# A hybrid decoder step: the FFN as one long up projection by seven block products for eight, activations through DRAM, and then a down projection in four blocks

## The chip, the cores and the metric

One Trainium2 chip, one core. The metric is the device time of one execution in microseconds. The kernel before takes 1333.52 us (median of 3 runs, 1333.43 to 1334.73).

## The reference, cut to what matters

One decoder layer over 16 meta tokens, 1024 prompt tokens and 8 x 4 sample tokens. The change is in its last two lines, the feed-forward network (FFN):

```python
D_MODEL = 1024; FFN_HIDDEN = 4 * D_MODEL          # all arrays float32
h = h + jnp.concatenate([y_a, y_b], axis=-1) @ w_out
u = jax.nn.relu(rmsnorm(h, norm_ffn) @ w_up)      # (tokens, 1024) @ (1024, 4096)
h = h + (u * u) @ w_down                          # (tokens, 4096) @ (4096, 1024)
y = rmsnorm(h, norm_final)                        # meta tokens dropped
```

Everything ahead of it (convolutions, gated delta rule, the product with `w_out`) is not touched, but for how the `w_out` stage hands `h` on.

## The kernel before, in words

Features lie on the 128 partitions, tokens along the free dimension: 1056 kept token columns (`KEPT`), or two halves of 528 (`HALF`), each of two parts of 264 (`PART`). A float32 product is made of three matmuls: every operand is split into a high part rounded to `float32r` (ScalarE, a copy) and a low part, the rest (a subtraction on VectorE or GpSimd), and TensorE adds high x high, high x low and low x high in PSUM. Each matmul has its own 128x128 weight load.

- `out_rows` (VectorE, L2611 on) adds the `w_out` product to `h` (`hT`), squares it into `h_squares`, and makes the low part `hg_low` of h times the norm's gain; `out_high` (ScalarE, L1297) makes `hg_high`.
- `sum_h` (TensorE, L1911), after the first unit of the FFN, adds the squares over the partitions into two banks for three column groups, so that its third group waits for VectorE's first `rstd_mid` (L2644). Then follow a square root (ScalarE L1309) and a reciprocal (VectorE L2647).
- Up projection (`up`, L1927 to L1929): 32 tiles of 128 hidden features, each over three column groups (288, 384, 384), 8 k-tiles x 3 matmuls in each. `up_rows` (VectorE, L2655, L2657) reads the bank, scales it by `h_squares`, and makes relu squared into `u_row`. 
- Down projection (`product`, L1945 to L1947): for 7 of 8 blocks of 4 hidden tiles it is done by Strassen-Winograd products: seven products instead of eight for each pair of output tiles (`PRODUCTS`; operands S of the weights, T of the activations). GpSimd makes the S sums (`pair_low`, L973 to L980) and the T sums (`make_t`, L954 to L960), ScalarE the high parts (L1325, L1334), VectorE the T low parts (L2661), GpSimd the weights' (L947, L966). `product_rows` (VectorE, L2676) adds each product to `hT`, 10 reads for 7 products. The last block goes without block products (`last_down`, L1963 to L1965), interleaved with transposes for the output.
- Order: each engine runs one list written out by hand. TensorE: up of blocks 0 and 1, then by turns the down products of block b and the up tiles of block b + 2 (`for b in range(NB - 1)`). Nothing of `u` leaves the chip's SBUF. SyncE's queue loads the weights, 512 KB each, through a ring; w_high and w_low hold eight sets of down weights.
- Counts in `acc_done`, `acc_read_dve`, `w_high`, `w_low` say when a unit's matmuls are done, a bank is read, and a weight set is ready; a queue waits in its order, and what stands behind a waiting instruction waits too.

Of the kernel before, what the change touches and what calls it, by code (L numbers as in the profile page):

```python
# [7 lines left out]
ALU = mybir.AluOpType  # L8
ACT = mybir.ActivationFunctionType
AX = mybir.AxisListType  # L10
F32 = mybir.dt.float32
# [34 lines left out]
FB = 4  # L46
NB = FFN // (FB * P)
HALF, PART = KEPT // 2, KEPT // 4
PAIRS = D // (2 * P)
PRODUCTS = [("A11", "B11", ((0, 0, 1), (1, 1, 1))), ("A12", "B21", ((0, 0, 1),)), ("S1", "T1", ((1, 0, -1), (1, 1, 1))),  # L50
            ("S2", "T2", ((1, 1, 1),)), ("S3", "T3", ((0, 1, -1), (1, 1, 1))), ("S4", "B22", ((0, 1, 1),)),
            ("A22", "T4", ((1, 0, 1),))]
READS = [len(x[2]) for x in PRODUCTS]
NP = len(PRODUCTS)
OPS = ("B11", "T1", "B21", "B22", "T2", "T3", "T4")
# [45 lines left out]
def build(nc, x_prompt, x_sample, state_conv_a, state_conv_qkv, state_ssm, meta_tokens, norm_mix, w_in,  # L101
# [4 lines left out]
    with ctx:  # L106
# [42 lines left out]
        hg_h = place("hg_high", [P, KT, TOK], F32R, R1)  # L149
        hg_l = place("hg_low", [P, KT, TOK], F32R, R1 + KT * SLOT)  # L150
        OPB = 2 * (FB // 2) * HALF * 4
        op_h = {x: place(f"op_high_{x}", [P, FB // 2, HALF], F32R, RK + OPB * i) for i, x in enumerate(OPS)}
        op_l = {x: place(f"op_low_{x}", [P, FB // 2, HALF], F32R, RK + OPB * i + OPB // 2) for i, x in enumerate(OPS)}
# [3 lines left out]
        w_pair = [place(f"w_pair{i}", [P, FB, 2 * P], F32, RING + 4096 * i) for i in range(2)]  # L157
# [103 lines left out]
        def scratch(name, shape):  # L261
# [8 lines left out]
        gate_d = scratch("gate_kept_rows", [NH, P, TOK])  # L270

# [3 lines left out]
        hsq = place("h_squares", [P, TOK], F32, RZ + NT * P * 4)  # L275
        ROW = KEPT * 4
        u_row = [place(f"u_row{i}", [P, KEPT], F32, a) for i, a in enumerate(
            [RK + NP * OPB, RK + NP * OPB + ROW, FREE, FREE + ROW, FREE + 2 * ROW, RZ])]
        assert NP * OPB + 2 * ROW <= 16 * SLOT and ROW <= NT * P * 4
        s_tmp = [place(f"w_sum{i}", [P, FB // 2, P], F32, FREE + 3 * ROW + 1024 * i) for i in range(2)]  # L280
        assert FREE + 3 * ROW + 2048 <= R1

        u_h = place("u_last_high", [P, FB, KEPT], F32R, R1)
        u_l = place("u_last_low", [P, FB, KEPT], F32R, R1 + FB * ROW)
# [98 lines left out]
        def has_last(n):  # L383
            return IN_TILES[n][0] in ("k", "q", "v", "H")

        N_LAST = sum(has_last(n) for n in range(N_IN))
        PER_UP, PER_DOWN = 3 * FB, NP * PAIRS
        DONE0, READ0 = 3 * N_MIX, dve_reads_to(N_MIX)

        def up_unit(b, i, m):  # L390
# [2393 lines left out]
```

## Time and profile before

| | us |
|---|---|
| median of 3 runs (lowest, highest) | 1333.52 (1333.43, 1334.73) |
| profiled execution: span, first to last instruction | 1329.9 |
| median less that span | 3.6 |
| FFN up to the first `last_down` matmul | 606.75 to 1267.62 |
| PE busy / DVE / POOL / ACT in the span | 1313.7 / 839.3 / 524.3 / 412.2 |

No time of its own is recorded for the profiled execution beyond its span; the runs are 3.6 us longer. Start times of rows are microseconds from the first instruction. A matmul's duration in a row is longer than its step to the next one, since matmuls overlap; the step between starts is what counts. A row's idle time is what its engine waited ahead of it. A row of windows reads: stretch, its length, busy time and instruction count of PE, PEld, DVE, ACT and POOL, granted clock, DMA share, GB/s. A row of groups reads: line, engine, operation, tiles, shape, count, busy us, mean ns, idle us ahead and what ended it. A row of a timeline reads: start, duration, engine, line, operation, tiles, shape, count.

### The profile page before, as it was taken

How to read it: one execution, taken by the hardware profiler on the slowest of the kernel's cores; microseconds unless marked ns; L12 is line 12 of the kernel's file. 1: busy time of each engine (PE TensorE's matmuls, PEld its weight loads, DVE VectorE, ACT ScalarE, POOL GpSimd, SP SyncE). 2: the span in 40 equal slices, each digit the busy share in tenths (PEclk: the TensorE clock that was granted, in tenths of full speed). 3: DMA queues.
4: the chain of work that ended last, by engine and by line, in shares of the span. 5: the costliest groups of instructions: out<-in, count | busy, mean ns of one | idle time of the engine just before them, and what ended most of it. 6: DMA issues, size and time to landing. Idle time of an engine off the chain costs nothing.

```text
span 1329.9 us, 22476 instructions
## 1 busy us (share of the span) xinstructions
PE 1313.7 (99%) x8984; PEld 1282.4 (96%) x8984; DVE 839.3 (63%) x1415; ACT 412.2 (31%) x806; POOL 524.3 (39%) x544
## 2 busy tenths in 40 slices
PE   7999999999999999999999999999999999999997
PEld 6899999899999999999999999999999999999997
DVE  6567898336453665556666756756667567566866
ACT  7566642112222213232122222322222223222313
POOL 1322112111111211221367466574574755746811
PEclk9999999999999999999999999999999999999999
DMA  6223554533323323221111212112121121111213
GB/s 193 71 66 90 163 179 77 185 115 88 88 64 85 99 57 90 81 65 48 48 33 48 64 33 63 34 48 64 33 59 54 34 63 48 49 49 32 81 39 124
DMA packets 161946, 99.88 MB, mean 75 GB/s; under 512 B 19735, under 2 KB 156467, under 8 KB 161842
## 3 DMA queue, kind: packets, MB, share of 16 engines
q1 hardware_dynamic: 138866, 85.56, 22.0%
q10 hardware_dynamic: 22976, 12.88, 3.6%
q8 instruction: 72, 1.18, 0.4%
q14 instruction: 32, 0.26, 0.1%
HBM read 77.62 MB, written 20.80 MB: 74 GB/s over the span
## 4 chain that ended last, share of the span: by engine, by line
PE 94%; DVE 3%; ACT 1%; issue 1%; DMA 1%; SPq 0%; POOLq 0%; POOL 0%; DVEq 0%; ACTq 0%
PE banks L1401 10%; PE banks L1403 9%; PE banks L1402 9%; PE banks L1927 9%; PE banks L1929 9%; PE banks L1928 9%; PE banks L1946 7%; PE banks L1947 7%; PE banks L1945 7%; PE banks L1963 1%; PE banks L1964 1%; PE banks L1965 1%; PE banks L1621 1%; PE banks L1635 1%; PE banks L1857 1%
## 5 line engine op out<-in xcount | busy, mean ns | idle before, releaser
L1927 PE MATMUL banks<-hg_high,w_high 128*128 128x384 f32 (+1 forms) x768 | 249.5, 325 | 0.0
L1929 PE MATMUL banks<-hg_high,w_low 128*128 128x384 f32 (+1 forms) x768 | 247.6, 322 | 0.0
L1928 PE MATMUL banks<-hg_low,w_high 128*128 128x384 f32 (+1 forms) x768 | 247.3, 322 | 0.0
L2676 DVE TENSOR_TENSOR hT<-hT,banks 128x528 f32<-128x528 f32 x280 | 189.4, 701 | 84.0 <-PE banks L1947 76.8
L1401 PE MATMUL banks<-xn_high,w_high 128*128 128x384 f32 (+1 forms) x672 | 227.3, 338 | 1.0 <-DVE xn_low L2059 0.9
L1403 PE MATMUL banks<-xn_high,w_low 128*128 128x384 f32 (+1 forms) x672 | 218.6, 325 | 0.0
L1402 PE MATMUL banks<-xn_low,w_high 128*128 128x384 f32 (+1 forms) x672 | 218.4, 325 | 0.0
L821 POOL TENSOR_TENSOR w_low<-w_raw,w_high 128x1024 fp32r<-128x1024 f32 x31 | 77.0, 2483 | 243.6 <-ACT w_high L1015 243.6
L1927 PEld LDWEIGHTS banks<-hg_high,w_high 128*128 128x128 f32 x768 | 144.2, 188 | 1.9 <-POOL w_low L947 1.7
L1928 PEld LDWEIGHTS banks<-hg_low,w_high 128*128 128x128 f32 x768 | 144.3, 188 | 0.1
L1929 PEld LDWEIGHTS banks<-hg_high,w_low 128*128 128x128 f32 x768 | 144.2, 188 | 0.0
L1401 PEld LDWEIGHTS banks<-xn_high,w_high 128*128 128x128 f32 x672 | 126.9, 189 | 3.6 <-DVE xn_low L2059 1.1
L966 POOL TENSOR_TENSOR w_low<-w_pair,w_high 128x256 fp32r<-128x256 f32 x140 | 104.1, 761 | 66.3 <-ACT w_high L1334 66.3
L2655 DVE TENSOR_TENSOR u_row<-banks,h_squares 128x384 f32<-128x384 f32 (+1 forms) x96 | 50.1, 522 | 126.4 <-PE banks L1929 126.2
L947 POOL TENSOR_TENSOR w_low<-w_raw,w_high 128x1024 fp32r<-128x1024 f32 x31 | 78.3, 2526 | 126.9 <-ACT w_high L1316 126.9
L1947 PE MATMUL banks<-op_high_T,w_low 128*128 128x264 f32 x448 | 127.7, 285 | 0.0
L1946 PE MATMUL banks<-op_low_T,w_high 128*128 128x264 f32 x448 | 127.7, 285 | 0.0
L1402 PEld LDWEIGHTS banks<-xn_low,w_high 128*128 128x128 f32 x672 | 127.2, 189 | 0.0
L1945 PE MATMUL banks<-op_high_T,w_high 128*128 128x264 f32 x448 | 127.1, 284 | 0.0
L1403 PEld LDWEIGHTS banks<-xn_high,w_low 128*128 128x128 f32 x672 | 126.6, 188 | 0.0
L1334 ACT ACTIVATE w_high<-w_pair 128x256 fp32r<-128x256 f32 x140 | 55.5, 415 | 177.5 <-PE banks L1929 84.3
L1947 PE MATMUL banks<-op_high_B,w_low 128*128 128x264 f32 x336 | 95.8, 285 | 0.0
(334 smaller groups left out, 2779.4 us busy)
## 6 DMA issues: line engine op xcount, KB each, us to landing
w_raw<-in_w_up SPq DMA_DIRECT2D x32, 512.0 KB, 4.1
w_pair<-in_w_down SPq DMA_DIRECT2D x32, 512.0 KB, 3.4
w_raw<-in_w_in SPq DMA_DIRECT2D x28, 512.0 KB, 4.0
w_raw<-in_w_out SPq DMA_DIRECT2D x8, 512.0 KB, 4.2
x_slice<-in_x_prompt SPq DMA_DIRECT2D x8, 512.0 KB, 4.3
out<-y_tok SPq DMA_DIRECT2D x8, 512.0 KB, 2.7
v_kept_rows<-v_feat SPq DMA_DIRECT2D x4, 536.0 KB, 2.9
gate_kept_rows<-gate_row SPq DMA_DIRECT2D x4, 536.0 KB, 3.3
```

What stands on the lines that cost most here:

```text
L947: pool.tensor_tensor(w_l[half][:, :, :], w_raw[n % 2][:, :, :], w_h[half][:, :, :].bitcast(F32), ALU.subtract).then_inc(w_low, 1)
L966: pool.tensor_tensor(set_of(w_l, b, s), set_source(n, PRODUCTS[x][0]), set_of(w_h, b, s).bitcast(F32), ALU.subtract).then_inc(w_low, 1)
L1401: pe.matmul(bank[:, 0:w], w_h[n % 2][:, k, :], hi[:, c0:c0 + w], start=(k == first), stop=False)
L1402: pe.matmul(bank[:, 0:w], w_h[n % 2][:, k, :], lo[:, c0:c0 + w], start=False, stop=False)
L1403: ins = pe.matmul(bank[:, 0:w], w_l[n % 2][:, k, :], hi[:, c0:c0 + w], start=False, stop=(k == last))
L1927: pe.matmul(bank[:, 0:w], w_h[half][:, k, :], hg_h[:, k, c0:c0 + w], start=(k == 0), stop=False)
L1928: pe.matmul(bank[:, 0:w], w_h[half][:, k, :], hg_l[:, k, c0:c0 + w], start=False, stop=False)
L1929: ins = pe.matmul(bank[:, 0:w], w_l[half][:, k, :], hg_h[:, k, c0:c0 + w], start=False, stop=(k == KT - 1))
L1945: pe.matmul(bank, high[:, j, :], op_h[name][:, j, cols], start=(j == 0), stop=False)
L1946: pe.matmul(bank, high[:, j, :], op_l[name][:, j, cols], start=False, stop=False)
L1947: ins = pe.matmul(bank, low[:, j, :], op_h[name][:, j, cols], start=False, stop=(j == FB // 2 - 1))
L2676: dve.tensor_tensor(hc, hc, both, ALU.add if sign > 0 else ALU.subtract).then_inc(acc_read_dve, 1)
```

## The change

Two phases. Up: all 16 pairs of hidden tiles by seven block products each (four k-tiles deep, 24 matmuls of 264 columns). Operands of h are made once at the start: `B11`, `B21`, `B22`, `T1` in the `w_out` stage, `T3`, `T2`, `T4` in turn after it, while pairs 0 and 1 run in the interleaved order `U_SEQ`. The results of pairs 0 to 13 are scaled, squared (ScalarE), turned into the seven operands of the down projection (VectorE) and sent to DRAM (SyncE). Down: block 0 of two pairs, blocks 1 to 3 of four, each product reading its operand back; pairs 14 and 15 stay and go to `last_down`. Weight sets: four, of up to four tiles, instead of eight of two.

```diff
+BLOCKS = ((0, 2), (2, 4), (6, 4), (10, 4))
+U_SEQ = ([(0, 0), (0, 1), (1, 0), (1, 1), (0, 4), (1, 4), (0, 6), (1, 6), (0, 2), (1, 2), (0, 3), (1, 3), (0, 5), (1, 5)]
+         + [(c, x) for c in range(2, UP_PAIRS) for x in range(NP)])
+FIRST_BANKS = (0, 1, 2, 3, 0, 2, 0, 2, 0, 2, 0, 2, 1, 3)
+CHAIN_BANK = (0, 1, 2, 3, 0, 1, 2)
+D_SEQ = ([(0, x, pair) for pair in range(PAIRS) for x in range(NP)]
+         + [(b, x, pair) for b in range(1, len(BLOCKS)) for x in range(NP) for pair in range(PAIRS)])
...
+        def set_free(s):
+            return DONE0 + s - 3 if s >= 4 else 3 * (N_MIX - 1 + s // 2)
...
 SyncE
+            for c in range(UP_PAIRS - 2):
+                send_row1(c)
...
+                send_row0(c)
+                send_turned(c)
+                if 2 <= c < UP_PAIRS - 3:
+                    sp.wait_ge(w_low, low_made(U_UNIT[c + 1, 6]))
+                    load_up(c + 3)
+            kept_pairs_sent()
+            load_part(0, 1)
+            sp.wait_ge(w_low, low_made(U_UNIT[UP_PAIRS - 2, 6]))
+            load_half(0)
+            for x in range(6):
+                load_first_op(x)
+            sp.wait_ge(w_low, low_made(U_UNIT[UP_PAIRS - 1, 6]))
+            load_part(0, 0)
+            load_first_op(6)
...
 GpSimd
+            up_low(1, 3)
+            up_low(0, 5)
+            for j in range(4):
+                turned_low(j)
+            up_low(1, 5)
+            for c in range(2, UP_PAIRS):
+                up_sum(c)
+                up_low(c, 0)
+                up_difference(c)
+                up_low(c, 1)
+                up_less_own(c)
+                for x in (2, 3, 4):
+                    up_low(c, x)
+                up_rest(c)
+                up_low(c, 5)
+                up_low(c, 6)
...
 ScalarE
+            last_half_scaled(0)
+            last_half_scaled(1)
+            up_set_high(1, 0)
+            last_half_scaled(2)
+            last_half_scaled(3)
...
+            up_set_high(1, 3)
+            turned_high("T4", 3)
+            up_set_high(0, 5)
+            up_set_high(1, 5)
...
 TensorE
+            def up(c, x):
+                u, name = U_UNIT[c, x], PRODUCTS[x][1]
+                if c == 0:
+                    if name == "T2":
+                        pe.wait_ge(w_low, low_made(T2_LOWS_AT) - 1)
+                    else:
+                        pe.wait_ge(low_s, UP_LOWS[name])
+                product(u, u, set_h[u % 4], set_l[u % 4], up_h[name], up_l[name], x >= 4 and not (c < 2 and x == 6))
...
 VectorE
+            turned_raw("T3", 0)
+            half_low("B22", N_OUT - 1, 1, 16)
+            turned_raw("T3", 1)
+            up_rows(0, 0)
+            for g in range(3):
+                mean_h(g)
+            up_rows(0, 1)
...
+            up_rows(0, 2)
+            turned_raw("T4", 3)
+            turned_low("T4", 0)
+            up_rows(1, 2)
...
+            root_inverse(2)
+            up_rows(1, 5)
+            right_whole(1)
+            root_inverse(3)
+            scale_row1(0)
+            scale_row0(0)
+            turn_u12(0)
+            turn_u34(0)
+            up_rows(2, 0)
```

`turned_raw` and `turned_low` are two-input operations on 528 columns. `up_rows` reads a product's two banks (528 columns) once, for x = 2 of pairs 0 and 1 twice. `scale_row1` and `scale_row0` take relu times `h_squares`, `turn_u12` and `turn_u34` make four operands of 528 columns. `change_basis` moves to pairs 4 to 7. `turned_low(j)` on GpSimd makes the four low parts of T2, `root_inverse(i)` a quarter of the reciprocal. `turned_low`, `up_low` and `down_low` count in one semaphore, `w_low`; `low_made(T2_LOWS_AT) - 1` is reached when sets 0 to 12 and the four T2 parts are made. Set 12 is that of (0, 5). In the down phase VectorE reads 10 times for seven products in blocks 1 to 3 and 7 times in block 0.

## Rows read from the trace of the kernel before

**Rows 1.** The page, sections 1 and 2: engines' busy time; granted clock by slice.
```profile
span 1329.9 us, 22476 instructions
PE 1313.7 (99%) x8984; PEld 1282.4 (96%) x8984; DVE 839.3 (63%) x1415; ACT 412.2 (31%) x806; POOL 524.3 (39%) x544
PEclk9999999999999999999999999999999999999999
```

**Rows 2.** Busy time by engine: FFN before its last block; one up block; one down block.
```profile
606.75:1267.80 661.05, 661.05 (x4665) 658.44 (x4664) 441.23 (x596) 178.52 (x335) 396.88 (x398) 1.00 0.17 50
742.50:788.95 46.45, 46.45 (x290) 46.20 (x289) 28.96 (x37) 12.89 (x21) 25.94 (x19) 1.00 0.14 43
701.43:742.50 41.07, 41.07 (x337) 41.07 (x337) 27.91 (x41) 10.77 (x25) 28.29 (x37) 1.00 0.19 55
```

**Rows 3.** Timeline of TensorE: matmuls of 384 and 264 columns, where an up block ends.
```profile
701.09 0.34 PE L1928 MATMUL banks<-hg_low,w_high 128*128 128x384 f32 x1
701.26 0.34 PE L1929 MATMUL banks<-hg_high,w_low 128*128 128x384 f32 x1
701.43 0.28 PE L1945 MATMUL banks<-op_high_B,w_high 128*128 128x264 f32 x1
701.55 0.28 PE L1946 MATMUL banks<-op_low_B,w_high 128*128 128x264 f32 x1
```

**Rows 4.** Timeline of TensorE at the FFN's start: the sum of squares.
```profile
609.95 2.11 PE L1911 MATMUL banks<-h_squares,one 128*128 128x288 f32 x6
611.60 0.63 PE L1927 MATMUL banks<-hg_high,w_high 128*128 128x384 f32 x1
```

**Rows 5.** Timeline of VectorE at the FFN's start.
```profile
606.95 0.55 DVE L2619 TENSOR_TENSOR hT<-hT,banks 128x384 f32<-128x384 f32 x1 [2.23 <-PE banks L1403]
608.14 0.56 DVE L2628 TENSOR_TENSOR h_squares<-h_squares,banks 128x384 f32<-128x384 f32 x1
610.63 0.46 DVE L2644 TENSOR_SCALAR h_squares<-banks 128x288 f32<-128x288 f32 x1 [1.41 <-PE banks L1911]
613.81 6.75 DVE L2647 RECIPROCAL h_squares<-h_squares 128x1056 f32<-128x1056 f32 x1 [1.16 <-ACT h_squares L1309]
```

**Rows 6.** Groups by line and shape, VectorE and ScalarE: busy us, mean ns | idle before.
```profile
L2676 DVE TENSOR_TENSOR hT<-hT,banks 128x528 f32<-128x528 f32 x280 | 189.4, 701 | 84.0 <-PE banks L1947 76.8
L2661 DVE TENSOR_TENSOR op_low_B<-u_row,op_high_B 128x528 fp32r<-128x528 f32 x42 | 28.2, 699 | 0.0
L2661 DVE TENSOR_TENSOR op_low_T<-u_row,op_high_T 128x528 fp32r<-128x528 f32 x56 | 81.5, 1476 | 2.8 <-ACT op_high_T L1325 2.8
L1325 ACT ACTIVATE op_high_T<-u_row 128x528 fp32r<-128x528 f32 x56 | 36.2, 647 | 143.4 <-POOL u_row L957 66.3 <-POOL u_row L954 51.1 <-POOL u_row L960 14.5
L1297 ACT ACTIVATE hg_high<-hT,tn 128x384 fp32r<-128x384 f32 x16 | 9.9, 618 | 54.2 <-DVE hT L2619 54.2
```

**Rows 7.** Groups by line and shape, GpSimd.
```profile
L966 POOL TENSOR_TENSOR w_low<-w_pair,w_high 128x256 fp32r<-128x256 f32 x140 | 104.1, 761 | 66.3 <-ACT w_high L1334 66.3
L957 POOL TENSOR_TENSOR u_row<-u_row,u_row 128x528 f32<-128x528 f32 x14 | 18.5, 1323 | 71.8 <-DVE op_low_B L2661 71.8
L960 POOL TENSOR_TENSOR u_row<-u_row 128x528 f32<-128x528 f32 x14 | 24.2, 1727 | 0.0
```

**Rows 8.** Timelines of VectorE and GpSimd: two VectorE additions beside one GpSimd subtraction; one alone.
```profile
633.10 3.52 DVE L2681 TENSOR_TENSOR hT<-hT 128x528 f32<-128x528 f32 x2
633.23 2.82 POOL L947 TENSOR_TENSOR w_low<-w_raw,w_high 128x1024 fp32r<-128x1024 f32 x1 [9.19 <-ACT w_high L1316]
743.90 2.39 POOL L947 TENSOR_TENSOR w_low<-w_raw,w_high 128x1024 fp32r<-128x1024 f32 x1 [3.47 <-ACT w_high L1316]
```

**Rows 9.** DMA: the queue's packets and share; issues with KB and us to landing.
```profile
q1 hardware_dynamic: 138866, 85.56, 22.0%
v_kept_rows<-v_feat SPq DMA_DIRECT2D x4, 536.0 KB, 2.9
x_tok<-in_x_prompt SPq DMA_DIRECT2D x1, 1024.0 KB, 8.3
```

More of the change, by code:

```diff
@@ new lines, in build, with parts_to, op_slot @@
+        for pair in range(PAIRS):
+            for i, name in enumerate(("S1", "S3", "S2", "S4")):
+                S_MADE[0, pair, name] = 4 * UP_PAIRS + 4 * pair + i + 1
+        for b in range(1, len(BLOCKS)):
+            for i, name in enumerate(("S1", "S3", "S2", "S4")):
+                for pair in range(PAIRS):
+                    S_MADE[b, pair, name] = 4 * UP_PAIRS + 4 * PAIRS * b + PAIRS * i + pair + 1
+        def parts_to(b):
+            return sum(n for _, n in BLOCKS[:b + 1])
+        def op_slot(o):
+            return 1 + (o - 1) % 4 if o else 0
@@ new lines, in load_part @@
+            def load_part(b, m):
+                k0, n = BLOCKS[b]
+                dst = ((w_down_12, w_down_22) if b else (w_first_12, w_first_22))[m]
+                sp.wait_ge(w_load[1], (A12_LOADED, A22_LOADED)[m][b] - 16 * n)
+                for j in range(n):
+                    sp.dma_start(dst[:, j, :, :], w_down_part_v[m, :, k0 + j, :, :]).then_inc(w_load[1], 16)
+            sp.wait_ge(w_low, N_MIX)
+            load_up(0)
+            load_up(1)
+            sp.wait_ge(w_low, low_made(U_UNIT[0, 5]))
@@ L998, in _ @@
+            for pair in range(PAIRS):
+                pool.wait_ge(w_high, high_made(LAST0 + pair))
+                pool.tensor_tensor(wx_l[pair][:, :, :], wx_raw[pair][:, :, :], wx_h[pair][:, :, :].bitcast(F32),
                                    ALU.subtract).then_inc(w_low, 1)
@@ L1360, in square_half @@
+            act.wait_ge(w_load[0], WX_LOADED)
+            for pair in range(PAIRS):
+                act.activation(wx_h[pair][:, :, :], wx_raw[pair][:, :, :], ACT.Copy).then_inc(w_high, 1)
             def square_half(r, half):
@@ L2690, in _, with down_rows @@
-            for i in range(FB):
-                for m in range(3):
-                    up_rows(0, i, m)
-                change_basis(i, ALU.subtract)
-            for b in range(NB - 1):
-                for c in range(PER_UP):
-                    up_rows(b + 1, c // 3, c % 3)
-                    if c < 2 * len(LOWS_AT):
-                        for name in LOWS_AT[c % 4]:
-                            op_low(b, c // 4, name)
-                for pair in range(PAIRS):
-                    for x in range(NP):
-                        product_rows(b, pair, x)
-                        if b == NB - 2 and pair and x in (0, 2, 4, 6):
-                            last_u_low(*LAST_LOWS[4 * (pair - 1) + x // 2])
+            def down_rows(b, x, pair):
+                u = D_UNIT[b, x, pair]
+                both = unit_pair(u)
+                dve.wait_ge(acc_done, done(u))
+                for mi, half, sign in (SINGLE_READS[x] if b else (CHAIN_READS[x],)):
+                    hc = split(quarter(pair, mi, half))
+                    dve.wait_ge(acc_read_dve, read(u - 1))
+                    dve.tensor_tensor(hc, hc, both, ALU.add if sign > 0 else ALU.subtract).then_inc(acc_read_dve, 1)
```

968 lines of the change are left out of this document (661 added, 307 removed).

## The prediction, made before the changed kernel ran

> **What bounds the kernel now.** I read the page's busy times first, then who waited for whom on TensorE, then the FFN's windows, then the timelines where stages meet. TensorE is busy 1313.7 of 1329.9 us, the next engine 839.3, and the granted clock is full in every slice [rows 1]. In the FFN up to its last block it is busy in 661.05 of 661.05 us [rows 2]: there the time is the number of matmuls times their step. Nothing else is on the path, so only two things count: how many steps the change removes, and which new waits open. The median is 3.6 us above the profiled span (1333.5 against 1329.9); I add the change to the median.
>
> **The up projection, removed and added.** An up block of four tiles takes 46.45 us [rows 2]; eight are 371.6 us (2304 matmuls of 352 columns on average). A down block of 336 matmuls of 264 columns takes 41.07 us [rows 2], a step of 122.2 ns, as neighbouring starts have it (701.43, 701.55 [rows 3]). The new up stage has 16 pairs x 7 products x 24 = 2688 matmuls of this same form: 328.6 us, 2.93 a product, 20.5 a pair. That is 43.0 us less. The down products are 7 x 28 x 12 before and 28 x 6 x (2 + 4 + 4 + 4) after, 2352 both times, at the same step: 0. The last block is the same: 0.
>
> Steps of 384 columns are 0.17 us, of 264 columns 0.12 [rows 3], so the time goes nearly by columns. The Trainium skill (TensorE: Matmul & The Clock Gate, "Back-to-back issue gap") has a rule that speaks against the change: a stream of weight load and matmul runs at about 81 ns at 128 columns and 131 at 512. An estimate on the line through that page's two figures is 110 ns at 352 columns and 99 at 264, and the up stage would grow by 11 us instead of shrinking by 43. The trace disagrees at both widths.
>
> **The start: three new waits.** Count from S, the first up product (606.75 before). Durations: a VectorE operation on 528 columns 0.70 [rows 6]; a high part on ScalarE 0.65, with a gain 0.75 (0.618 at 384 columns [rows 6], scaled up); GpSimd 1.32 at 528 columns, 0.76 at 256 [rows 7], so 1.29 at 512.
>
> (a) sum_h. Before, VectorE takes up the mean (L2644) 0.68 us after the sum began, and the sum costs TensorE 611.60 - 609.95 = 1.65 us [rows 4, 5]. After, VectorE finishes the last squares at S + 1.95 (608.70 [rows 5]), then has T3's first part (ready for it at S + 2.3, after two ScalarE operations with gain), the last low part of B22, T3's second part and up_rows(0, 0) ahead of the mean: four at 0.70 to 0.76, till S + 5.3. The mean takes 0.46; the third sum starts at 5.8 to 6.3, and the next product at about 6.8 instead of 2.93 + 1.65 = 4.6. Cost 2.2; ends 0 and 4 (all four beside GpSimd).
>
> (b) T2's low parts. Product 10, (0, 3), waits for weight set 12 and behind it four GpSimd operations. From the end of product 8: up_rows(0, 2) reads twice (1.4), T4's last raw part (0.7), its high part on ScalarE (0.65), set 12's high part queued behind it (0.65), its low part (1.3), the four T2 parts (5.3): 10.0 us, plus 0.7 to 1.5 for VectorE's T4 low parts in between (next paragraph). Product 9 covers 2.93. Cost 7.1 to 8.6; I take 7.8. Nothing else covers it: products 11 to 13 stand behind 10 in TensorE's list.
>
> (c) VectorE's backlog after it. Behind up_rows(1, 5) come right_whole (0.7), a quarter of the reciprocal (6.75 / 4 = 1.7 [rows 5]), two scalings of 1056 columns (1.4 each), ScalarE's square (1.1), four turns (2.8), and only then up_rows(2, 0), 10 us if undisturbed; the piece ahead, a quarter of the reciprocal before up_rows(1, 5), adds 0.9. Product (2, 4) needs that bank read, 4 x 2.93 = 11.7 us after product (1, 5). With nothing in the way it just fits (0); with GpSimd in the way of seven operations at 0.6 it is 4 late. I take 2.5.
>
> **The port, or what VectorE and GpSimd share.** Two VectorE additions of two SBUF inputs, 0.70 each undisturbed, take 3.52 beside a GpSimd subtraction that takes 2.82 where it takes 2.39 alone [rows 8]; together they last as long as their sum (3.8). VectorE's T low parts, made while GpSimd works, have a mean of 1.476 against 0.699 [rows 6]; operations with one input in PSUM keep 0.701 with GpSimd busy 28 of 41 us [rows 2, 6]. So these two kinds exclude each other, and their times add. An up pair needs 11 GpSimd operations at 1.29 (14.2) and on VectorE four turns and two scalings (six operations, 4.9): 19.1 of 20.5 us, and 20.5 in pairs 4 to 7 with change_basis. TensorE is not held: a set may be late by three products (8.8) less its own 0.65 and 1.29, 6.9 us. Cost 0; the far end is the third rival.
>
> The Trainium skill (SBUF — State Buffer, "Who interferes with whom") says the same more sharply: with two SBUF inputs on VectorE and a GpSimd read the second to issue is blocked for the other's whole instruction. By it GpSimd would be stopped up to 1.4 us by the long scaling and the pair's sum would stay 19.1; by plain sharing of bandwidth it would be less. The rows fit the rule, and by both TensorE isn't held.
>
> VectorE alone in a pair: seven reads (4.9), 4.9, six waits of up to 1.3: at most 17.6 of 20.5. ScalarE: 7 x 0.65 + 2 x 1.1 = 6.8. SyncE: load_up(c + 3) is queued behind the sends of pair c, which end about product (c + 1, 4); 1 MB lands within 8.3 us [rows 9], still some 10 us before GpSimd wants it. DRAM traffic of a pair is 7 x 0.27 + 1.05 = 2.9 MB in 20.5 us, 141 GB/s; a queue's packets move 85.56 MB in 22.0% of the span, 292 GB/s when all engines move [rows 9]. Hidden.
>
> **The turn to the down phase.** From 3 us before the last pair begins to 12 us into it SyncE issues 5.8 MB (weights of block 0, seven operands of 0.54 MB). At 292 GB/s they end at +17 to +20, and the last operand is wanted by ScalarE at +22, the first at +12. Cost 0; at the slowest rate of [rows 9] (1 MB in 8.3 us, 126 GB/s) it would be 46 us, some 20 late. Nearer is the 536 KB in 2.9 us (189 GB/s): 31 us, hence 5 late. I take 1. Block 1 crowds the port: GpSimd has 8 operations in four products for x = 0, 1, 2, 4 (10.3), VectorE a low part of 2 x 1.4, and in block 1 two scalings (x = 0) and last_u_low (x = 4, 5) besides, so x = 0 needs 15.9 of 11.7 us, x = 1 and 2 13.1 each. The lag grows to 7.0 against the 6.9 allowed. I take 1; ends 0 and 5. Block 0 has GpSimd at 44 x 0.77 = 34 of 41 us as now, with half as many sets ahead (4.4 us less 1.2): 0.
>
> **Sum.** -43.0 + 2.2 + 7.8 + 2.5 + 1 + 1 = -28.5. Time 1305.0.
>
> **Rivals.**
> 1. The waits at the start overlap with what they delay (VectorE catches up during (b), and the backlog (c) and sum_h go away): only (b), 7.1, remains: 1333.5 - 43.0 + 7.1 = 1297.6; with nothing at all 1290.5. For it: VectorE idles for 8 us in (b). Against: (c) comes after, and depends on (b)'s products, not on work that could be done in (b).
> 2. The turn or block 1 costs much more: 5 and 5 instead of 2, up to 20: 1313 to 1323. For it: SyncE's list waits in order; the trace never shows 5.8 MB at once. Against: 292 GB/s in the packets.
> 3. Slower: the port binds the whole up stage. If GpSimd's 11 operations last 1.67 (1.727 at 528 columns [rows 7]) and VectorE's 4.9 still come on top, a pair takes 23.3 us, 2.8 over TensorE, in 14 pairs 39 us: 1305.0 + 39 = 1344. It decides from 2.0 us over (22.5 a pair). Against: the 1.727 has VectorE's share in it already; 1.323 is the undisturbed row.
> 4. TensorE's step doesn't fall with the width in the up stage. By the estimate from the skill's line the time would be 1333.5 + 11 + 14.5 = 1359. Worked from rows it would take a step of 161 ns (371.6 / 2304) at 264 columns, where they show 122: 1410.
> 5. The change doesn't do what it says, as the seven products need more than counted: the diff has 24 matmuls in each, and no others are added; I see nothing for it.
>
> **Chances.** Forecast 0.62 (its own range 1299 to 1313); rival 1 0.13; rival 2 0.16; rival 3 0.06; rival 4 0.01; between them, within 0.2% of before, 0.02. 0.2% (2.7 us) is about what a measurement of this kernel can tell from no change. Faster 0.91, same 0.02, slower 0.07. Range 1293 to 1322: it leaves out the part of rival 1 with no stall, the end of rival 2, and 3 and 4.
>
> **What would show it.** Right: windows over pairs 3 to 13 with TensorE busy throughout at 20.5 us a pair, a step of 0.122; TensorE idle 2 us in sum_h until the mean, 7 to 9 us before (0, 3) until GpSimd's low part of T2, and a few us before (2, 4) until VectorE's read. Wrong: idle TensorE in every pair waiting for w_low (rival 3), a gap of over 5 us before the first down product until a DMA (rival 2), no gap before (0, 3). A span not 3.6 us below the median would spoil the sum.

## The result, and the profile after

| | before | after |
|---|---|---|
| median (lowest, highest), us | 1334.12 (1333.43, 1335.76), 4 runs | 1309.43 (1306.9, 1309.83), 4 runs |
| profiled execution: its time / its span | - / 1329.9 | 1306.9 / 1305.1 |
| first FFN product to first `last_down` | 606.75 to 1267.62: 660.9 | 607.27 to 1242.60: 635.3 |
| of this, the up stage | eight blocks, 371.6 in all, without `sum_h` | 607.27 to 956.11: 348.8, with `sum_h` |

The ratio is 0.9821, 95% interval 0.9805 to 0.9837. The span fell by 24.8 us. In what follows "up stretch" is the time from the first up product to the first down product (348.8 us here); the start of the FFN moves by some 5 us between profiled executions for reasons ahead of it, so the stretch compares kernels more finely than the span. It is read from one execution of each kernel, and what the clock costs behind one and the same gap differs between executions by up to 1.4 us (see the end), so differences of 1 or 2 us between stretches say little. Line numbers are those of the changed kernel; an experiment's can differ by a few.

The page of the changed kernel, for the lines of [rows 1] and [rows 9]:

```profile
span 1305.1 us, 23215 instructions
PE 1273.1 (98%) x9368; PEld 1242.6 (95%) x9368; DVE 816.0 (63%) x1257; ACT 463.9 (36%) x772; POOL 664.9 (51%) x504
PEclk9999999999999999999989999999999999999999
q1 hardware_dynamic: 141778, 138.55, 33.0%
```

TensorE is no longer busy throughout: 1305.1 - 1273.1 leaves 32 us, against 16.2 before, and one slice has a lower clock. GpSimd gained 140.6 us. The view of who waited for whom on TensorE, of the changed kernel, gives the new idle time (total, times, longest):

```profile
PE banks L2229 <- POOL up_low_T L1110: 8.4, 1, 8.4
PE banks L2214 <- DVE h_squares L2999: 3.8, 1, 3.8
PE banks L2229 <- DVE u_rows L3023: 3.1, 1, 3.1
```

They are the three waits (b), (a) and (c) of the prediction, 15.3 us together. All other waits on TensorE in the FFN are 0.4 us or less: none in the later pairs, none before the first down product. The windows of the changed kernel (columns as in [rows 2]) show the up stretch, the down blocks, and a part of the up stage far from its ends:

```profile
607.27:956.11 348.84, 333.61 (x2695) 331.89 (x2695) 234.21 (x245) 120.52 (x169) 284.85 (x183) 0.98 0.40 137
956.11:1242.60 286.49, 286.29 (x2354) 285.91 (x2353) 179.40 (x199) 112.37 (x141) 250.99 (x175) 1.00 0.39 132
740.00:945.00 205.00, 205.00 (x1691) 205.00 (x1690) 125.51 (x137) 65.55 (x92) 175.04 (x111) 1.00 0.44 152
616.00:620.00 4.00, 4.00 (x22) 3.69 (x21) 0.56 (x1) 1.31 (x2) 1.84 (x2) 0.63 0.00 0
652.00:656.00 4.00, 3.62 (x16) 3.62 (x17) 0.00 (x0) 0.00 (x0) 2.79 (x3) 0.50 0.31 69
680.00:684.00 4.00, 3.13 (x15) 3.16 (x16) 3.69 (x6) 0.00 (x0) 2.48 (x2) 0.57 0.18 68
```

From 740 to 945 TensorE is busy 205.00 of 205.00 us, with GpSimd busy 85% of the time. The last three rows are the stretches behind the three gaps. There the granted clock is 0.50 to 0.63, and the timeline of TensorE shows what this means for the step (answering to [rows 3], where it was 0.12):

```profile
652.38 0.59 PE L2229 MATMUL banks<-up_high_T,set_high 128*128 128x264 f32 x1 [8.38 <-POOL up_low_T L1110]
652.77 0.42 PE L2231 MATMUL banks<-up_low_T,set_high 128*128 128x264 f32 x1
652.99 0.42 PE L2232 MATMUL banks<-up_high_T,set_low 128*128 128x264 f32 x1
```

A step of 0.22 us instead of 0.12: TensorE works at the lower of its two levels, 1.2 GHz, after it stood idle. I counted the steps over 0.18 us behind each gap: they last 2.2, 4.1 and 3.0 us, and are 1.0, 1.9 and 1.4 us longer than the same steps at 2.4 GHz, 4.3 us in all. Behind (a) this leaves out the last two matmuls of `sum_h` and the step that follows them: they take 0.61, 0.07 and 0.79 us, and 0.43, 0.03 and 0.42 in run 1, where this gap is gone. That is 0.6 us more.

The timelines of VectorE and GpSimd at the FFN's start, for [rows 5], show why (a) was longer than forecast. VectorE:

```profile
608.06 1.41 DVE L2932 TENSOR_TENSOR banks<-hT 128x384 f32<-128x384 f32 x1
609.97 0.76 DVE L2977 SCALAR_TENSOR_TENSOR up_raw_T<-hT,tn,up_raw_T 128x528 f32<-128x528 f32 x1
610.65 1.83 DVE L2943 SCALAR_TENSOR_TENSOR up_low_B<-hT,tn,up_high_B 128x528 fp32r<-128x528 f32 x1
612.40 1.85 DVE L2977 SCALAR_TENSOR_TENSOR up_raw_T<-hT,tn,up_raw_T 128x528 f32<-128x528 f32 x1
614.17 0.69 DVE L3023 COPY u_rows<-banks 128x528 f32<-128x528 f32 x1
614.79 0.90 DVE L2999 TENSOR_SCALAR h_squares<-banks 128x288 f32<-128x288 f32 x2
```

GpSimd:

```profile
607.74 1.30 POOL L1089 TENSOR_TENSOR w_up_sum<-w_up_sum,w_up_raw 128x512 f32<-128x512 f32 x1
610.65 1.27 POOL L1103 TENSOR_TENSOR set_low<-w_up_raw,set_high 128x512 fp32r<-128x512 f32 x1 [1.60 <-ACT set_high L1531]
612.42 1.27 POOL L1103 TENSOR_TENSOR set_low<-w_up_sum,set_high 128x512 fp32r<-128x512 f32 x1 [0.50 <-ACT set_high L1531]
```

The operation of L2977 takes 0.76 us alone and 1.85 when a GpSimd operation runs. The mean, which the forecast had at S + 5.3 us, begins at S + 7.5.

The timeline of GpSimd in gap (b), and of VectorE ahead of gap (c):

```profile
645.11 1.27 POOL L1103 TENSOR_TENSOR set_low<-w_up_raw,set_high 128x512 fp32r<-128x512 f32 x1 [1.84 <-ACT set_high L1531]
646.34 5.99 POOL L1110 TENSOR_TENSOR up_low_T<-up_raw_T,up_high_T 128x528 fp32r<-128x528 f32 x4
```

```profile
670.70 1.26 DVE L3060 SCALAR_TENSOR_TENSOR u_rows<-u_rows,h_squares 128x1056 f32<-128x1056 f32 x1
671.88 1.25 DVE L3066 SCALAR_TENSOR_TENSOR u_rows<-u_rows,h_squares 128x1056 f32<-128x1056 f32 x1
674.28 0.71 DVE L3072 TENSOR_TENSOR u_rows<-u_rows 128x528 f32<-128x528 f32 x1 [1.16 <-ACT u_rows L1586]
675.03 1.68 DVE L3076 TENSOR_TENSOR u_T<-u_rows 128x528 f32<-128x528 f32 x1
676.75 1.67 DVE L3080 TENSOR_TENSOR u_T<-u_rows,u_T 128x528 f32<-128x528 f32 x1
678.34 1.76 DVE L3081 TENSOR_TENSOR u_T<-u_rows,u_T 128x528 f32<-128x528 f32 x1
680.03 0.69 DVE L3023 COPY u_rows<-banks 128x528 f32<-128x528 f32 x1
```

The groups of VectorE in the up stage, of the changed kernel by line and shape (columns as in [rows 6]), set the two kinds of operation side by side:

```profile
L3081 DVE TENSOR_TENSOR u_T<-u_rows,u_T 128x528 f32<-128x528 f32 x14 | 25.1, 1790 | 0.0
L3026 DVE TENSOR_TENSOR u_rows<-u_rows,banks 128x528 f32<-128x528 f32 x32 | 22.5, 703 | 50.7 <-PE banks L2232 50.4
```

With both inputs in SBUF the mean of this operation is 1790 ns, with one in PSUM 703. L3081 is the kind that meets a GpSimd operation in every pair; the other operations of a pair with 528 columns and both inputs in SBUF have means of 746 (L3072), 771 (L3066), 1259 (L3080) and 1616 ns (L3076). Set 12 is ready at 646.4, but product (0, 3) waits for the four T2 parts until 652.3. And (2, 4) waits for the copy at 680.03, behind three turned operands that take 1.7 to 1.8 us each, not 0.7.

### The profile page after: what moved, and what is told of

Same layout as the page of the kernel before. It is cut to its first block, busy times and chain, and to the rows that moved or that the text cites. A ratio compares the mean times of both kernels' runs of the same rounds, so it can differ in the third digit from the quotient of the medians.

```text
span 1305.1 us, 23215 instructions
## 1 busy us (share of the span) xinstructions
PE 1273.1 (98%) x9368; PEld 1242.6 (95%) x9368; DVE 816.0 (63%) x1257; ACT 463.9 (36%) x772; POOL 664.9 (51%) x504
## 3 DMA queue, kind: packets, MB, share of 16 engines
q8 instruction: 75, 1.23, 0.4%
## 4 chain that ended last, share of the span: by engine, by line
PE 87%; DVE 6%; issue 3%; ACT 1%; POOL 1%; DMA 1%; SPq 0%; POOLq 0%; DVEq 0%; ACTq 0%
PE banks L2229 14%; PE banks L2232 14%; PE banks L2231 14%; PE banks L1704 10%; PE banks L1706 10%; PE banks L1705 10%; PE banks L2271 1%; PE banks L2272 1%; PE banks L2273 1%; PE banks L1924 1%; PE banks L1938 1%; POOL set_low L1103 1%; PE banks L2160 1%; DMA w_raw<-in_w_in 1%; DVE hT L3100 1%
## 5 line engine op out<-in xcount | busy, mean ns | idle before, releaser
L2229 PE MATMUL banks<-op_high,set_high 128*128 128x264 f32 x672 | 191.2, 285 | 0.2
L2232 PE MATMUL banks<-op_high,set_low 128*128 128x264 f32 x672 | 190.8, 284 | 0.0
L2231 PE MATMUL banks<-op_low,set_high 128*128 128x264 f32 x672 | 190.5, 283 | 0.0
L2229 PE MATMUL banks<-up_high_T,set_high 128*128 128x264 f32 x512 | 147.7, 288 | 8.4 <-POOL up_low_T L1110 8.4
L1103 POOL TENSOR_TENSOR set_low<-w_up_raw,set_high 128x512 fp32r<-128x512 f32 x80 | 124.5, 1557 | 54.2 <-ACT set_high L1531 54.0
L2232 PE MATMUL banks<-up_high_T,set_low 128*128 128x264 f32 x512 | 146.6, 286 | 0.0
L2231 PE MATMUL banks<-up_low_T,set_high 128*128 128x264 f32 x512 | 146.4, 286 | 0.0
L2229 PEld LDWEIGHTS banks<-op_high,set_high 128*128 128x128 f32 x672 | 126.3, 188 | 0.6 <-DVE op_low L3110 0.3
L2232 PEld LDWEIGHTS banks<-op_high,set_low 128*128 128x128 f32 x672 | 126.4, 188 | 0.0
L2231 PEld LDWEIGHTS banks<-op_low,set_high 128*128 128x128 f32 x672 | 126.3, 188 | 0.0
```

Of the source, the lines that this page charges most:

```text
L1103: pool.tensor_tensor(set_l[s % 4][:, :, :], up_source_at(s), set_h[s % 4][:, :, :].bitcast(F32), ALU.subtract).then_inc(w_low, 1)
L2229: pe.matmul(bank, high[:, j, :], op_high[:, j, cols], start=(j == 0 and not begun), stop=False, skip_group_check=True)
L2231: pe.matmul(bank, high[:, j, :], op_low[:, j, cols], start=False, stop=False, skip_group_check=True)
L2232: ins = pe.matmul(bank, low[:, j, :], op_high[:, j, cols], start=False, stop=(j == n - 1), skip_group_check=True)
```

## The experiments

All are built on the changed kernel, and timed beside the kernel before (1332.5 to 1333.3 us in these runs). Ratios are to the kernel before. Where nothing else is said, only the order of the same work changes.

**1. The means first** (`e1_mean_first`).

```diff
             turned_raw("T3", 0)
+            mean_h(0)
+            mean_h(1)
             half_low("B22", N_OUT - 1, 1, 16)
+            mean_h(2)
             turned_raw("T3", 1)
             up_rows(0, 0)
-            for g in range(3):
-                mean_h(g)
```

> VectorE takes the three means of the squares (mean_h) right after T3's first part, ahead of the last low part of B22, T3's second part and up_rows(0, 0). Theory (what stands ahead of the mean in VectorE's list costs TensorE the 3.8 us gap): the gap falls under 0.7 us, as before the change, the slow clock after it (0.63 from 616 to 620) goes too, and the time falls by 4 to 5 us, to about 1305. Rival (VectorE's total work in this stretch is the bound, it is busy 36 of its first 41 us): the 3.8 us come back as waits for its reads or low parts before the product (0, 3), and the time stays at 1309, within 1 us.

Measured: 1303.77 us, ratio 0.9782 (0.9767 to 0.9796), up stretch 344.6. The wait for `h_squares` is gone from the list; (b) is 8.7 and (c) 3.1. So wait (a) was VectorE's order alone, and it isn't taken over by another.

**2. T2's low parts early** (`e2_t2_lows_early`): the first behind set 10's low half, the others behind set 11's; `T2_LOWS_AT` and `low_made` count accordingly, and T4's last raw part goes ahead of `up_rows(0, 2)`.

```diff
             up_low(1, 2)
+            turned_low(0)
             up_low(0, 3)
+            for j in range(1, 4):
+                turned_low(j)
             up_low(1, 3)
             up_low(0, 5)
-            for j in range(4):
-                turned_low(j)
```

> GpSimd makes T2's four low parts between weight sets 9 and 11 instead of behind set 12, and VectorE makes T4's last raw part before up_rows(0, 2) instead of behind it. Theory (the chain behind set 12 makes the 8.4 us gap): the last T2 low part ends about 646.5 instead of 652.3, the gap before (0, 3) falls to 2 to 3 us, and with less half-speed time behind it the time falls by 6 to 8 us, to about 1302. Rival (GpSimd's and VectorE's joint work sets the end of this stretch, whatever the order): the gap is cut up and turns up before (1, 3), (0, 5) and (2, 4); the time falls by less than 2 us.

Measured: 1303.76 us, ratio 0.9777 (0.9761 to 0.9793), up stretch 344.4. (b) falls from 8.4 to 2.7, (c) grows from 3.1 to 4.0: counted from the first up product, TensorE comes to (2, 4) 6.2 us sooner than in the changed kernel, and VectorE's copy only 5.3.

**3. The four quarters of the reciprocal ahead of `up_rows(0, 3)`** (`e3_reciprocals_early`).

```diff
             turned_low("T4", 2)
+            for i in range(4):
+                root_inverse(i)
             up_rows(0, 3)
             turned_low("T4", 3)
-            root_inverse(0)
...
```

> The four quarters of the reciprocal (1.8 us each) stand ahead of up_rows(0, 3), where VectorE is idle for 8.8 us, instead of between the later reads. Theory (VectorE's backlog behind product (1, 5) makes the 3.1 us gap before (2, 4)): the gap goes, with it the clock of 0.57 behind it, and the time falls by 4 to 5 us, to about 1305. Rival (the gap is the chain of scaling, ScalarE's square and the turns, with or without the reciprocals): the gap stays over 2 us and the time within 1 us.

Measured: 1303.8 us, ratio 0.9784 (0.9767 to 0.9802), up stretch 345.5. (c) is 1.0 and no slow stretch follows it. VectorE does this work while TensorE stands in gap (b), which rival 1 of the prediction had said could be done and I had argued against.

**4. Gap (b) filled** (`e4_filled_gap`): the work is that of the changed kernel, with 60 matmuls that no result needs.

```diff
                     if name == "T2":
+                        pe.wait_ge(acc_read_dve, banks_read_before(u))
+                        for i in range(60):
+                            pe.matmul(ps[UNIT_BANKS[u][i % 2]][:, 0:PART], up_h["B11"][:, i % 4, 0:P], up_h["B11"][:, i % 4, 0:PART],
+                                      start=True, stop=True, skip_group_check=True)
                         pe.wait_ge(w_low, low_made(T2_LOWS_AT) - 1)
```

> Before it waits for T2's low parts, TensorE makes 60 matmuls of 264 columns into the bank that the next product clears, 7.3 us of work of no use inside the 8.4 us gap. Theory (the clock falls because TensorE is idle, and costs some 2 us at half speed after the gap): the step behind the gap is 0.122 us from the first matmul on instead of 0.22, and the time falls by 2 us, to about 1307.4. Rival (the slow start is not the idleness but the wait itself): the step is 0.22 for 4 us again and the time stays within 0.5 us of 1309.4; if the 60 matmuls last longer than the gap, it grows.

Measured: 1306.58 us, ratio 0.9808 (0.9788 to 0.9827); up stretch 349.4, not shorter than 348.8. The idle time at (b) is 1.1 us. Its windows show that the clock was kept there (compare 652 to 656 above):

```profile
650.00:655.00 5.00, 5.00 (x43) 5.00 (x42) 3.19 (x3) 0.03 (x1) 5.00 (x4) 1.00 0.58 192
655.00:660.00 5.00, 3.89 (x32) 3.67 (x32) 0.00 (x0) 0.00 (x0) 4.41 (x4) 1.00 0.16 44
```

But the slow stretches behind (a) and (c), which weren't touched, were longer in this execution: 4.0 and 5.6 us, costing 1.8 and 2.6 instead of 1.0 and 1.4. The profiled execution was the longest of the four, 1310.89 us at a mean granted clock of 0.990; the others took 1307.58 (0.991), 1305.58 and 1304.95 (0.995 both). In the profiled one the saving was lost at the other gaps, so this run shows that a busy TensorE keeps its clock, and doesn't show that this saves time. Runs 10 and 11 were made for that.

**5. Runs 1 and 2 together** (`e5_mean_and_t2`).

> Both reorderings together: the mean first, and T2's low parts between sets 9 and 11. Each alone shortened the stretch from the first up product to the first down product by 4.2 and 4.4 us (344.6 and 344.4 against 348.8). Theory (queue order): they add, 340 to 341 us, and the time is about 1301. Rival (VectorE's work sets the stretch once the gaps are small: it would be busy some 37 of 37 us before (0, 3)): the second gives less than half of its 4.4 us, the stretch stays over 342 and new waits for VectorE's reads or low parts come before (0, 2) or (2, 4).

Measured: 1298.76 us, ratio 0.9743 (0.9723 to 0.9763), up stretch 340.3: the gains add. (b) 3.9, (c) 3.9.

**6. All three** (`e6_all_three`).

> The same with the four quarters of the reciprocal ahead of up_rows(0, 3) as well. Alone that gave 3.3 us, in VectorE's idle time, which is gone here for the most part. Theory: the 7.2 us of reciprocals now delay up_rows(0, 3) and T4's last low part, so (0, 5) waits 2 to 4 us, and the wait before (2, 4) falls by as much: 340 us, no better than without it, within 1 us. Rival (there is slack between the reads): 337 us, 3 us faster.

Measured: 1303.44 us, ratio 0.977 (0.9748 to 0.9792), up stretch 342.6, worse than without the third. The waits on TensorE in the up stretch:

```profile
PE banks L2230 <- DVE up_low_T L2994: 5.1, 1, 5.1
PE banks L2230 <- POOL up_low_T L1110: 3.9, 1, 3.9
PE banks L2230 <- DVE u_rows L3024: 1.0, 1, 1.0
```

With gap (b) cut to half, VectorE's idle time there is too short for 7.2 us of reciprocals (its timeline has it busy without a pause, the four quarters from 648.89 to 656.2); they push T4's last low part, and (0, 5) waits for it. What was free in run 3 costs 5.1 us here, more than the 2 to 4 expected, and (c) falls by 2.9 only.

**7. Is GpSimd and VectorE's shared port near its limit?** (`e7_three_more_on_gpsimd`): three of the eleven GpSimd operations of each pair from 2 on are made twice, the first copy overwritten by the second.

```diff
+                if c >= 2 and x in (0, 2, 4):
+                    pool.tensor_tensor(set_l[s % 4][:, :, :], up_source_at(s), set_h[s % 4][:, :, :].bitcast(F32),
+                                       ALU.subtract).then_inc(again, 1)
+                    pool.wait_ge(again, 3 * (c - 2) + (0, 2, 4).index(x) + 1)
```

> From pair 2 on GpSimd makes three of a pair's seven low parts twice (the same 512 columns, the second one counts): 3 x 1.3 us a pair more, with nothing else changed. Theory (a GpSimd operation and a two-SBUF-input operation of VectorE exclude each other, so 14 x 1.29 + 4.9 = 23 us are wanted of 20.5): TensorE waits for set_low in every pair, 2.0 to 2.5 us, and the up stage grows by 26 to 35 us; time about 1340. Rival (they only share bandwidth; GpSimd alone is busy 18.1 of 20.5): no wait in any pair, time within 2 us of the changed kernel's 1309.

Measured: 1325.99 us, ratio 0.9947 (0.9932 to 0.9962), up stretch 364.6, 15.8 more than the changed kernel. It lies between the two theories. The window of this kernel:

```profile
740.00:945.00 205.00, 197.97 (x1600) 195.03 (x1599) 134.43 (x130) 60.50 (x87) 202.73 (x135) 1.00 0.38 133
```

and a line of its waits on TensorE:

```profile
PE banks L2233 <- POOL set_low L1107: 9.3, 17, 0.9
```

GpSimd works back to back (202.73 of 205) and sets the pace: 21.2 us a pair in its timeline, 22.0 in pairs with `change_basis`. Fourteen operations at 1.28 are 17.9 us, so VectorE's six two-input operations take 3.3 us of GpSimd's time, not the 4.9 that my sum gave them. The real load of the changed kernel's pair is then 11 x 1.28 + 3.3 = 17.4 of 20.4 us, which its window bears out (175.04 of 205.00), and rival 3 was further away than I thought.

The single rows show where the difference comes from. These three, of the timelines of GpSimd and VectorE of the changed kernel, stand here in order of time:

```profile
806.07 1.75 POOL L1103 TENSOR_TENSOR set_low<-w_up_raw,set_high 128x512 fp32r<-128x512 f32 x1
806.59 1.79 DVE L3081 TENSOR_TENSOR u_T<-u_rows,u_T 128x528 f32<-128x528 f32 x1
807.78 1.76 POOL L1093 TENSOR_TENSOR w_up_raw<-w_up_raw 128x512 f32<-128x512 f32 x1
```

VectorE's operation takes 1.79 us instead of 0.70: it loses 1.09 of the 1.23 us that the first GpSimd operation still had to run. The second GpSimd operation takes 1.76 instead of 1.28: it loses 0.48 of the 0.60 us that VectorE's still had. From 740 to 945 us, in this kernel and in run 7, either engine loses on average what is left of the other's operation, less 0.13 us. So the two kinds do exclude each other, and the first theory had the price too high: a GpSimd operation is held for 0.48 us, and not for the whole 0.70 of VectorE's row. [rows 8] had shown it, with 3.52 us for what adds up to 3.8.

The Trainium skill (SBUF — State Buffer, "Who interferes with whom") has the second to issue blocked for the other's whole instruction. The rows of both engines fit this but for the 0.13 us. With whole rows the rule gives 23 us a pair (17.9 + 4.9, an estimate), and this run shows 21.2.

**8. Is the DRAM traffic hidden?** (`e8_sent_twice`): every operand of pairs 0 to 13 is sent to DRAM twice, the first time to a second area that nobody reads.

```diff
+                for to in (op_e, op_d):
+                    sp.dma_start(to[b][2:4, :, j, :].rearrange("o p c -> p o c"),
+                                 u_buf[c % 2][:, 1, :].rearrange("p (o c) -> p o c", o=2)).then_inc(spill_sent[c % 2], 16)
...
```

> Every activation operand is sent to DRAM twice, first to a second place that is never read, on the same queue, and the buffers are released when both are there: 26.5 MB more, 4.8 MB instead of 2.9 MB in a pair's 20.5 us. Theory (the trip through DRAM is hidden with room to spare): no new wait on TensorE, time within 1.5 us of 1309.4. Rival (the sends hold the buffers and stand ahead of the weight loads in SyncE's list, near the limit): load_up comes late, GpSimd waits for w_up_raw, and TensorE loses over 1 us in every pair, 15 us or more in all.

Measured: 1309.25 us, ratio 0.9822 (0.9803 to 0.9842), as without it; up stretch 350.7, of whose 1.9 more 1.6 are what longer slow stretches behind the same three gaps cost (5.9 us against 4.3). The window, beside that of the changed kernel (0.44, 152):

```profile
740.00:945.00 205.00, 205.00 (x1691) 205.00 (x1691) 125.54 (x137) 66.09 (x92) 175.36 (x111) 1.00 0.66 236
```

26.5 MB more are moved with no new wait of TensorE.

**9. Only two quarters of the reciprocal early** (`e9_two_quarters_early`), on top of run 5.

```diff
             turned_low("T4", 2)
+            turned_low("T4", 3)
+            root_inverse(0)
+            root_inverse(1)
             up_rows(0, 3)
-            turned_low("T4", 3)
-            root_inverse(0)
             up_rows(1, 3)
-            root_inverse(1)
```

> Means first and T2's low parts early (as e5_mean_and_t2), and of the four quarters of the reciprocal only the first two ahead of the copies out for (0, 3) and (1, 3); the third and fourth stay where they were. If VectorE's list is only too long by the two operations of 1.8 us that lie just ahead of the turn to pair 2, the gap of 3.9 us before (2, 4) goes to under 1 us and no new wait comes before (0, 5) (in e6_all_three it was 5.1 us), the 3.9 us for T2's low parts stay: up stretch 340.3 - 3 to 5 = 335 to 337 us, time 1294 to 1296. If the moved time comes back as another wait of the same size (the list is full in this stretch, wherever the operations stand), the stretch stays at 339 to 342 and the time at 1298 to 1302.

Measured: 1299.83 us, ratio 0.9751 (0.9736 to 0.9765), up stretch 340.4, as run 5 (340.3). The first theory fell: (c) is 4.1 us, not under 1. In VectorE's timeline the first scaling of pair 0 begins 54.2 us after the first up product, in run 5 after 54.0. Its pauses before it shrank from 1.6 to 0.4 us, but T4's last low part, moved to where GpSimd is busy, takes 1.8 us instead of 0.7. The stretch is full, and moving a piece within it changes nothing at its end.

**10 and 11. The clock** (`e10_gap_in_each_pair`, `e11_same_gap_filled`).

The second kernel is shown; the first has the condition and the last line alone.

```diff
+                if 2 <= c < UP_PAIRS - 1 and x == 3:
+                    pe.wait_ge(acc_read_dve, banks_read_before(u))
+                    for i in range(22):
+                        pe.matmul(ps[UNIT_BANKS[u][i % 2]][:, 0:PART], up_h["B11"][:, i % 4, 0:P], up_h["B11"][:, i % 4, 0:PART],
+                                  start=True, stop=True, skip_group_check=True)
+                    pe.wait_ge(w_low, low_made(U_UNIT[c, x] + 3))
```

> The changed kernel, with one more wait of TensorE in each of the twelve pairs 2 to 13: before its fourth product it waits until the low half of the set three products later is made, which GpSimd can only begin when the product before has freed that buffer, so some 2 to 3.5 us of idle time each, 24 to 42 us in all. If TensorE works at half speed for 2 to 5 us after each such gap (theory: the clock is the term that my sum lacked, 1.0 to 2.6 us a gap), the time rises by the idle time plus 12 to 31 us, and the steps after the gaps show 0.22 us instead of 0.122. If the slow steps after the three gaps of the changed kernel belonged to their place (first use of the tiles), the time rises by the idle time alone and the steps stay at 0.122.

> As e10_gap_in_each_pair, with 22 matmuls that no result needs (128x264 columns, into the banks of the coming product, 0.122 us each = 2.7 us) issued ahead of the added wait. TensorE is held back as long as before but isn't idle for most of it. If the cost beyond the idle time is the clock's, it is gone here: steps 0.122 throughout, and the kernel is faster than e10_gap_in_each_pair by 12 to 31 us, though the wait is the same. If it comes from anything else (the ring of set buffers run empty, GpSimd thrown off its lead), both kernels take the same time to within 4 us.

Measured: 1357.36 us (ratio 1.0179, 1.0162 to 1.0196) with the gaps, 1348.68 us (1.0113, 1.0097 to 1.0128) with the gaps filled. Up stretches 399.5 and 388.7. The added waits are 34.8 us (37.9 less the 3.1 that (c) had) in the first kernel. (The condition holds for thirteen pairs, 2 to 14, not the twelve of the expectation.) The slow steps cost 17.1 us in the first kernel and 5.4 in the second, where they stand behind (a), (b) and the gap in pair 2 only, which the 22 matmuls cover in part. So idle time plus clock is 34.8 + 12.8 = 47.6 of the 50.7 us that the stretch grew by; and filling brings 10.8 us in the stretch, 8.7 in the medians. This is less than the 12 to 31 expected, because not every gap lowers the clock. Two gaps of the first kernel, in its timeline of TensorE:

```profile
857.24 0.59 PE L2229 MATMUL banks<-up_high_T,set_high 128*128 128x264 f32 x1 [2.54 <-POOL set_low L1103]
857.62 0.42 PE L2231 MATMUL banks<-up_low_T,set_high 128*128 128x264 f32 x1
857.84 0.42 PE L2232 MATMUL banks<-up_high_T,set_low 128*128 128x264 f32 x1
...
881.84 0.39 PE L2229 MATMUL banks<-up_high_T,set_high 128*128 128x264 f32 x1 [2.54 <-POOL set_low L1103]
882.06 0.29 PE L2231 MATMUL banks<-up_low_T,set_high 128*128 128x264 f32 x1
882.19 0.28 PE L2232 MATMUL banks<-up_high_T,set_low 128*128 128x264 f32 x1
```

and the windows behind them:

```profile
857.20:860.50 3.30, 3.27 (x15) 3.27 (x16) 0.55 (x1) 0.00 (x0) 1.68 (x1) 0.52 0.57 220
881.80:885.10 3.30, 3.27 (x26) 3.27 (x27) 0.58 (x2) 0.00 (x0) 1.69 (x1) 1.00 0.57 220
```

The same 2.54 us of idle time, the same place in the pair: behind one the clock is 0.52 for 3.2 us, which costs 1.5 us, behind the next it is 1.00 and costs nothing. The added gaps of 6.35 and 3.68 us in pairs 2 and 3 were both followed by slow steps (2.7 and 2.8 us of cost), and so were six of the eleven gaps of 2.54 us (1.4 to 1.5 each). The rival, that slow steps belong to the first use of the tiles, has fallen: they come in the middle of the stage, and go when the gap is filled.

**12. What TensorE waits for ahead of what a DMA waits for** (`e12_copies_before_turns`), on top of run 5.

```diff
             turn_u12(0)
-            turn_u34(0)
+            dve.wait_ge(turned_s, 18)
             up_rows(2, 0)
             up_rows(2, 1)
+            turn_u34(0)
             up_rows(2, 2)
```

> e5_mean_and_t2 with one more change of order in VectorE's list: the copy out for (2, 0) and the subtraction for (2, 1) stand ahead of the two turned operands T3 and T4 of pair 0 (1.65 and 1.76 us in e5_mean_and_t2), with a wait that T2, which reads the same rows, is made. e9_two_quarters_early showed that VectorE's list has no slack up to this point, so work ahead of it can't be shifted within it; what can be done is to put what TensorE waits for before what only a DMA waits for. If the 3.9 us before (2, 4) are the 3.4 us of these two operations, the gap goes to 0.5 to 1 us and its half-speed stretch (2.3 us) goes with it: stretch 340.3 - 3.4 - 2.3 = 334 to 336 us, time 1293 to 1295. If VectorE is simply behind here, the next copies, now behind the turns, are late for (2, 6) or (3, 0) instead: a wait of 2 to 4 us appears there, and the stretch stays at 339 to 341, the time at 1298 to 1300.

Measured: 1298.07 us (5 runs, 1293.63 to 1300.02), ratio 0.9722 (0.9704 to 0.9741), up stretch 338.4. Gap (c) went from 3.9 to 0.6 us, as the first theory has it, and no slow steps are left behind it; no wait of 2 to 4 us came for VectorE. Yet the stretch fell by 1.9 only, not by 4 to 6: three waits for GpSimd's `set_low` came (1.5 us together), and the slow stretch behind (b) was 5.9 us long instead of 3.0 (2.7 us of cost against 1.4). The forecasts of 334 to 336 us for the stretch and 1293 to 1295 for the time were missed, and in the medians the kernel can't be told from run 5. Both beat the changed kernel by some 11 us.

## Why the prediction was right, point by point

**Fewer steps, -43.0: right, and 2.3 better.** 2688 up matmuls come at 121.4 ns (mean over neighbouring starts in the up stretch, those behind gaps left out): 326.3 us, so -45.3. The same 264-column steps were 122.2 ns in the down blocks before, and are 121.5 there now, which is why the down phase takes 286.5 us instead of 287.5. I took the old step for the new stage. Why it is 0.6% shorter I haven't tested. The rule of the Trainium skill (TensorE: Matmul & The Clock Gate, "Back-to-back issue gap") that made rival 4 doesn't hold here: the trace has 121.4 ns at 264 columns, where an estimate on the line through its figures gives 99.

**(a) sum_h, +2.2: measured 3.8 idle, near the upper end of 4, and 4.4 with the half-speed matmuls of the sum itself.** The order of four operations ahead of the mean was right. The size wasn't: I gave each 0.70 to 0.76 and kept "all four beside GpSimd" for the bound; two of them, and one of the squares before, did meet GpSimd and took 1.85, 1.83 and 1.41. The squares ended at S + 2.8 instead of 1.95. Run 1 shows that the wait comes from this order.

**(b) T2's low parts, +7.8: measured 8.4**, within 7.1 to 8.6. The four parts took 5.99 us, not 5.3. Run 2 takes most of it away.

**(c) VectorE's backlog, +2.5: measured 3.1.** "With GpSimd in the way of seven operations at 0.6" was the mechanism (its terms add up to 3.4 us late, not 4): the three last turns take 1.7 to 1.8 each, the reciprocal's quarters 1.80. Runs 3 and 12 take it away in two ways.

**The turn and block 1, +2: measured 0.** From 690 to 1242 us the view of waits has none on TensorE that it lists (the down blocks' idle time is 0.20 us in all by the window); block 1 was worked out with the same too heavy price for GpSimd. The turn's 1 us went by 189 GB/s; in the windows from 935 to 945 and 945 to 956 us the queues move 304 and 296 GB/s, and TensorE is busy throughout.

**The port in the up stage, 0: right**, though "their times add" is 0.13 us too much each time one engine holds the other; run 7 gives 17.4 of 20.4 us where I had 19.1. It also shows how near the edge is: three more operations a pair cost 15.8 us. **The transfers, 0: right**, with room for 26.5 MB more (run 8).

**What was missing: the clock.** No term stood for it; the kernel before never stops TensorE in the FFN, and its profile shows full clock in every slice [rows 1]. Each gap of 3 us or more in the changed kernel was followed by half-speed steps, 4.3 us in all. The sum for the stretch up to the last block is now -45.3 + 3.8 + 8.4 + 3.1 + 4.3 - 1.0 = -26.7, against -25.5 measured (660.9 to 635.3). Of the 1.2 us between them 0.6 are the half-speed matmuls of `sum_h`. Another 0.4 are a matter of counting: an idle time begins at a matmul's end, 0.28 us after its start in the rows, and the next would have started after 0.12. The FFN began 0.5 us later and the last block took 0.2 more, which makes the span's -24.8. That the forecast of -28.5 came within 3.8 us of the medians' -24.7 is in part chance: the waits were 2.8 us too small and the clock missing, and against that the steps were 3.3 us (2.3 in the up stage, 1.0 in the down blocks) and the turn 2 us too dear.

**Rival 1** (the waits overlap) had a true core: in run 3 VectorE does the reciprocals in gap (b) for nothing. The kernel as written doesn't use it, since its list has them behind. **Last step, the bookkeeping:** the 3.6 us between median and span mixed two executions. Every execution on record takes 1.8 to 1.9 us more than its own span; the rest was the difference between the profiled execution and the median. As the change was added to the median, the forecast doesn't depend on it; but "a span not 3.6 us below the median" was no sign of anything: it is 4.3 here (1309.43 less 1305.1).

## What to carry to other kernels

When a stage gains from fewer steps, look for the cost where its queues start, not in its steady part: the three waits of the changed kernel came in full or for the most part from an engine's written order, where something nobody was waiting for stood ahead of what TensorE needed. Price a VectorE operation of 528 columns with two SBUF inputs at up to 1.8 us instead of 0.7 where it meets a GpSimd operation, and an idle gap of TensorE of 2.5 us or more at its length plus 0 to 2.8 us of half-speed steps; gaps of 1.1 us or less had none here. Gains from gaps add as long as the engine behind them has idle time; once it hasn't (runs 6 and 9), moving its work only moves the wait. A change of what comes first (run 12) took the wait away, though the time could not be told from run 5's.

## What the runs showed of the hardware that I had not expected

- After a gap TensorE's steps take 0.22 us instead of 0.12 for 1 to 6 us, and what this costs differs from execution to execution for the same gap: 0.5 to 1.9 us behind (a), 1.4 to 2.6 behind (c) where it is 3 us or more. Behind equal gaps of 2.54 us, one pair after the other, it came or stayed away. What decides it these runs don't show. A TensorE kept busy with matmuls without use kept its clock (runs 4 and 11).
- An operation of GpSimd and one of VectorE with both inputs in SBUF exclude each other: whichever comes second loses what is left of the first, less 0.13 us. VectorE's 0.70 becomes up to 1.79 and GpSimd's 1.28 becomes 1.76. VectorE's operations with one input in PSUM keep 0.70 with GpSimd busy 85% of the time.
- A reciprocal of 264 columns takes 1.80 us, 6.8 ns a column, where other VectorE operations of 528 columns take 0.70.
